# A delta-net stage: U of both blocks made ahead of A, gate decays of the third and last head and one SiLU moved

## Chip, cores and metric

The kernel runs on one core of a Trainium2 chip. The metric is the device time of one execution in microseconds (us). The work is one program with an instruction stream for each engine: TensorE (PE), VectorE (DVE), ScalarE (ACT), GpSimd (POOL) and SyncE (SP). They meet only at semaphores.

## What is computed

Two transformer blocks over 512 tokens of width 1024, all in float32. The change touches only the second block's gated delta rule: 8 heads, key width 128, value width 256, over 528 tokens (16 meta tokens are put ahead). The kernel uses chunks of 128 tokens where the reference has 64, which gives the same result.

```python
def gated_delta_rule(q, k, v, g, beta):
    g = jnp.cumsum(to_chunks(g), axis=-1)
    incl, strict = idx[:, None] >= idx[None, :], idx[:, None] > idx[None, :]
    decay = jnp.exp(jnp.where(incl, g[..., :, None] - g[..., None, :], -jnp.inf))
    kb = k * beta[..., None]
    lower = jnp.where(strict, jnp.einsum('nbhid,nbhjd->nbhij', kb, k) * decay, 0.0)
    rhs = jnp.concatenate([v * beta[..., None], kb * jnp.exp(g)[..., None]], axis=-1)
    sol = lax.linalg.triangular_solve(eye + lower, rhs, left_side=True, lower=True)
    u, w = sol[..., :DV], sol[..., DV:]
    attn = jnp.einsum('nbhid,nbhjd->nbhij', q, k) * decay
    ...
    def step(S, xs):
        v_new = u_c - jnp.einsum('bhcd,bhde->bhce', w_c, S)
        o = einsum(qd_c, S) + einsum(attn_c, v_new)
        S = S * gl_c[..., None, None] + einsum(kd_c, v_new)
        return S, o

# in hybrid_mixer
q = l2norm(heads(jax.nn.silu(causal_depthwise_conv(dq, conv_q)), DN_DK))
k = l2norm(heads(jax.nn.silu(causal_depthwise_conv(dk, conv_k)), DN_DK))
v = heads(jax.nn.silu(causal_depthwise_conv(dv, conv_v)), DN_DV)
o_dn = rmsnorm_2(o_dn, dn_gain) * jax.nn.silu(heads(dz, DN_DV))
```

## The kernel before

**Weights.** Every weight matrix is read from memory in units of 128 output columns. ScalarE rounds a unit to its high part (`w_hi`), VectorE, or in this stage GpSimd, subtracts that from the raw weights (`w_lo`), and TensorE makes three products for each of 8 input tiles. One such input tile is an event ("mm", 8 of them a unit); its six matmuls take about 0.73 us. These products are the bulk of the time, and the delta work is laid between them. Whenever a unit's last tile is issued, ScalarE and GpSimd prepare the unit four further on.

**The order.** `delta_order` (L162) writes the order of events by hand: tables such as `PREPARE`, `DECAYS`, `SCAN`, `L2_FIRST` give each step of a head a time, counted in us of TensorE work (`WORK`, L103) for `steps` and in fill events for `after`, and `timed` (L116) merges them with the product tiles. All engines walk through the same list `DELTA` and each takes its own part of an event, so the list fixes the order on every engine; semaphores do the rest. Iteration i of the loop (0 to 8) scans head i, prepares head i+1, and makes the gate decay and the normed q and k of head i+2.

**A head's preparation.** "bcast" (L2012): ScalarE waits until GpSimd has done with `gB` and `r3` of the head before and issues two DMAs that spread a gate row over 128 partitions. "decay": ScalarE (L2021) makes five Relus, two Exps into `DT`, one Exp of `gB` and a small copy to `gl`; VectorE (L2752) multiplies `DT` by a 0/1 mask (two steps); GpSimd (L3115) makes `LT` from `DT` and the spread row (two steps). "pair" : TensorE (L1380) multiplies k by k and q by k chunk by chunk, first the four chunks of 128 tokens, then the tail of 16; VectorE (L2758) makes from them `UT`, the start of the inverse, and `AT`, the attention matrix. "turn": TensorE (L1395) transposes `UT` of the four chunks, then of the tail; ScalarE copies both back. "x1" to "x6" and "u1" to "u6" double the inverted blocks, with GpSimd making the masked `LM` (L3121), the first right behind "turn".

**A head's scan.** "v0" to "v4" make the new values of a chunk on TensorE, and ScalarE copies them to `V`; "s0" to "s4" update the state `S` and the output; "k1" to "k4" apply the state. "nsq", "norm", "gain0", "gain1", "parts" norm the output and multiply it with SiLU(z), "hiz" splits it in high and low (`oh` on ScalarE, `ol` on GpSimd) for the branch products. "siluqk", "siluv", "siluz" are ScalarE's SiLUs, of which the first after an Exp loads an activation table. `stk0` to `stk2` are VectorE's steps of the norm of k; TensorE waits at "pair" for the last of them. z is kept once, so ScalarE's copy of the next head's z out of PSUM waits until "parts" of this one is done.

**PSUM.** A planner (`Banks.delta`, L969) walks the list too. The chain's small products take four banks in turn from a `Ring` (L413); with each use it notes the semaphore value that tells that the bank's content was read, and the next user of the bank waits for that value beside its own waits. `s.p_u` counts VectorE's eight steps in `pairs` of a head. The product of k and k of the four chunks is ("pair", h, 0), that of q and k ("pair", h, 1), both of the tail are in ("pair", h, 2). In heads 1 to 6 the ring gives ("turn", h, 0) the bank of ("pair", h, 1) and ("turn", h, 1) that of ("pair", h, 2). Head 0 and head 7 fall otherwise: there the transposes take banks that were free before, or that of ("pair", h, 0). The units of products have two pairs of banks of their own, used in turn.

## Time and profile before

| | us |
|---|---|
| median of 3 runs | 2822.25 |
| lowest and highest run | 2819.61, 2822.37 |
| profiled execution, its own time | 2817.93 |
| its span, first to last instruction | 2816.1 |
| delta stage in it | about 1305 to 2000 |
| TensorE busy | 2732.6 (97%) |
| VectorE, ScalarE, GpSimd busy | 1532.0, 1144.8, 472.7 |
| mean granted clock of TensorE | 0.99 |

Times in rows are us from the start of the span unless marked ns. "PE" is TensorE's matmuls, "PEld" its weight loads. A row of a timeline gives start and length; rows that follow one another with the same tiles are merged, and the count stands behind the x. In brackets stands how long the engine was idle before and what ended that. Nearly every VectorE and ScalarE step is recorded by a helper (L481, L486, L492, L474), so the tiles tell which step a row is, out<-in. Granted clock (PEclk) is a share of full speed: 1.00 is 2.4 GHz, 0.50 is 1.2 GHz.

### The profile page before, as it was taken

To read this page: it belongs to the slowest core of one execution; us is meant where nothing else is said; L and a number is where in the kernel's file an instruction comes from. 1 tells how busy PE (TensorE), PEld (TensorE's weight loads), DVE (VectorE), ACT (ScalarE), POOL (GpSimd) and SP (SyncE) were. 2 spreads that over 40 slices of the span, in tenths; PEclk is the share of its full clock that TensorE was granted. 3 is DMA by queue.
4 is the path that set the end of the run, shared out by engine and by line. 5 is a ranking of instruction groups with operands and counts; after the bars stand their busy time and mean duration, and the time that the engine had idled before them with its cause. 6 is when DMAs were issued, how large, how long until landed. Compare 5 with 4: busy or idle time off the path is not lost.

```text
span 2816.1 us, 37383 instructions
## 1 busy us (share of the span) xinstructions
PE 2732.6 (97%) x14573; PEld 2226.4 (79%) x14573; DVE 1532.0 (54%) x2165; ACT 1144.8 (41%) x1709; POOL 472.7 (17%) x278
## 2 busy tenths in 40 slices
PE   8999999998999999998999999999999999999999
PEld 3888888886666788887888888878878877788887
DVE  6735637348667433337645555663367765644443
ACT  4221211226554422235654645554366663432221
POOL 0000000011001000003434444443322222100000
PEclk9999999999999999999999999999999999999999
DMA  6423424222114232323211121211211112332332
GB/s 237 154 88 104 135 75 135 86 67 90 38 46 158 83 98 89 98 90 103 75 40 53 46 68 61 61 48 44 81 55 60 55 60 101 91 100 94 92 101 77
DMA packets 69873, 241.80 MB, mean 86 GB/s; under 512 B 8218, under 2 KB 8346, under 8 KB 69314
## 3 DMA queue, kind: packets, MB, share of 16 engines
q1 hardware_dynamic: 62032, 221.28, 24.6%
q10 hardware_dynamic: 7666, 18.13, 1.9%
q8 instruction: 117, 1.92, 0.3%
q14 instruction: 58, 0.48, 0.1%
HBM read 232.74 MB, written 6.64 MB: 85 GB/s over the span
## 4 chain that ended last, share of the span: by engine, by line
PE 85%; DVE 7%; ACT 6%; issue 1%; DMA 1%; ACTq 0%; DVEq 0%; POOL 0%; SPq 0%; POOLq 0%
PE ps L1115 62%; PE ps L1517 3%; PE ps L1414 2%; PE ps L1618 2%; PE ps L1454 2%; PE ps L1321 1%; PE ps L1342 1%; PE ps L1446 1%; ACT r L474 1%; DVE UT L481 1%; PE ps L1145 1%; ACT w_hi L474 1%; PE ps L1154 1%; DVE f_t L492 1%; PE ps L1475 1%
## 5 line engine op out<-in xcount | busy, mean ns | idle before, releaser
L1115 PE MATMUL ps<-Nh,w_hi 128*128 128x512 f32 (+1 forms) x1808 | 661.3, 366 | 9.6 <-DVE Nl L481 4.9
L1115 PE MATMUL ps<-Nl,w_hi 128*128 128x512 f32 (+1 forms) x1808 | 631.2, 349 | 0.0
L1115 PE MATMUL ps<-Nh,w_lo 128*128 128x512 f32 (+1 forms) x1808 | 628.8, 348 | 0.0
L474 ACT ACTIVATE w_hi<-w_raw 128x1024 fp32r<-128x1024 f32 (+1 forms) x352 | 368.2, 1046 | 633.2 <-PE ps L1115 465.3
L481 DVE TENSOR_TENSOR w_lo<-w_raw,w_hi 128x1024 fp32r<-128x1024 f32 (+1 forms) x242 | 297.7, 1230 | 260.9 <-ACT w_hi L474 250.8
L1115 PEld LDWEIGHTS ps<-Nh,w_hi 128*128 128x128 f32 x1808 | 343.1, 190 | 80.1 <-issue 30.2
L1115 PEld LDWEIGHTS ps<-Nl,w_hi 128*128 128x128 f32 x1808 | 343.4, 190 | 50.6 <-issue 5.8
L1115 PEld LDWEIGHTS ps<-Nh,w_lo 128*128 128x128 f32 x1808 | 343.4, 190 | 44.3
L481 POOL TENSOR_TENSOR w_lo<-w_raw,w_hi 128x1024 fp32r<-128x1024 f32 x110 | 270.4, 2458 | 608.0 <-ACT w_hi L474 604.2
L1115 PE MATMUL ps<-x1h,w_hi 128*128 128x512 f32 (+1 forms) x784 | 272.7, 348 | 11.9 <-ACT x1h L474 8.7
L1115 PE MATMUL ps<-x1l,w_hi 128*128 128x512 f32 (+1 forms) x784 | 267.1, 341 | 0.0
L1115 PE MATMUL ps<-x1h,w_lo 128*128 128x512 f32 (+1 forms) x784 | 265.4, 339 | 0.0
L1115 PEld LDWEIGHTS ps<-x1h,w_hi 128*128 128x128 f32 x784 | 147.5, 188 | 44.4 <-issue 20.9
L1115 PEld LDWEIGHTS ps<-x1l,w_hi 128*128 128x128 f32 x784 | 147.8, 189 | 18.4 <-issue 1.4
L1115 PEld LDWEIGHTS ps<-x1h,w_lo 128*128 128x128 f32 x784 | 147.9, 189 | 18.2 <-DVE w_lo L481 0.2
L481 POOL TENSOR_TENSOR f_t<-f_t,f_t 128x768 f32<-128x768 f32 (+1 forms) x12 | 22.4, 1868 | 658.4 <-ACT f_t L474 658.4
L492 DVE SCALAR_TENSOR_TENSOR ada_acc<-w_raw,sc,ada_acc 128x512 f32<-128x512 f32 x168 | 126.3, 752 | 8.8 <-DVE X L492 0.5
L1115 PE MATMUL ps<-h1h,w_hi 128*128 128x512 f32 x352 | 119.1, 338 | 0.0
L1115 PE MATMUL ps<-h1l,w_hi 128*128 128x512 f32 x352 | 118.9, 338 | 0.0
L1115 PE MATMUL ps<-h1h,w_lo 128*128 128x512 f32 x352 | 117.9, 335 | 0.0
L481 DVE TENSOR_TENSOR f_t<-f_t,ps 128x768 f32<-128x768 f32 (+1 forms) x44 | 36.1, 821 | 141.3 <-PE ps L1115 140.8
L474 ACT ACTIVATE f_t<-ps 128x768 f32<-128x768 f32 (+1 forms) x44 | 31.0, 705 | 150.4 <-PE ps L1115 149.7
(364 smaller groups left out, 4645.1 us busy)
## 6 DMA issues: line engine op xcount, KB each, us to landing
w_raw<-in_w_in SPq DMA_DIRECT2D x132, 512.0 KB, 3.5
w_raw<-in_w_proj SPq DMA_DIRECT2D x89, 512.0 KB, 3.5
w_raw<-in_w_ada SPq DMA_DIRECT2D x52, 512.0 KB, 4.3
w_raw<-in_w_out SPq DMA_DIRECT2D x48, 448.0 KB, 3.3
w_raw<-in_w_out SPq DMA_DIRECT2D x24, 512.0 KB, 3.5
w_raw<-in_w_mix_in SPq DMA_DIRECT2D x19, 512.0 KB, 3.5
w_raw<-in_w_bdn SPq DMA_DIRECT2D x16, 512.0 KB, 3.5
w_raw<-in_w_mix_out SPq DMA_DIRECT2D x8, 512.0 KB, 3.5
```

The source lines that it names most:

```text
L474: self.then_inc(self.e.activation(out, in_, func, **kw), sem)
L481: self.then_inc(self.e.tensor_tensor(out, a, b, op), sem)
L492: self.then_inc(self.e.scalar_tensor_tensor(out=out, in0=a, scalar=s, in1=b, op0=op0, op1=op1), sem)
L1115: ins = e.matmul(out[:, 512 * j:512 * j + n], a[:, kk, :], x[:, kk, c0:c0 + n], start=k == 0 and p == 0, stop=k == nt - 1 and p == 2)
L1145: ins = e.matmul(bank[0:2, 0:512], t.sc[:, 2 * k:2 * k + 2], a[:, i, :], start=k == 0, stop=k == KT - 1)
L1154: ins = e.matmul(bank[0:2, 0:512], t.pick[:, 2 * v:2 * v + 2], t.ada_acc[:, u, v, :], start=v == 0, stop=v == 1)
L1321: ins = e.matmul(out, a[:, k, :], x[:, k, 0:TX], start=k == 0 and p == 0, stop=k == KT - 1 and p == 2)
L1342: ins = e.matmul(out, a[:, kk, :], x, start=i % 4 == 0 and p == 0, stop=i % 4 == 3 and p == 2)
L1414: ins = e.matmul(bank[0:n, c * n:(c + 1) * n], t.LM[lv % 2][0:n, c0 + c, 0:n], UT[0:n, 1, c0 + c, 0:n], start=True, stop=True)
L1454: ins = e.matmul(out, t.Xm[0:n, c0 + c, 0:n], block_columns(UT[0:n, 0, c0 + c, 0:n], lv, 1), start=True, stop=True)
L1517: ins = e.matmul(out[:, 0:TX], a[:, 2 * (k % 4) + x, :], b[:, x, MS], start=x == 0 and p == 0, stop=x == 1 and p == 2)
L1618: ins = e.matmul(out[:, 0:TX], a[:, k, :], b[:, 0, MS], start=p == 0, stop=p == 2)
```

## The change

In `pairs` VectorE makes `UT` of the four chunks and of the tail first, and `AT` of both behind that. The counts that others wait for follow: the transposes and `LM` wait for 8h+3 and 8h+6 or 8h+1 and 8h+4 instead of 8h+7 and 8h+5 for the tail; in the bank plan the release of ("pair", h, 1) goes from value 8h+4 to 8h+7.

The event "decay" is split: "decay" is ScalarE's part alone, and the new event "mask" is VectorE's and GpSimd's. In most heads both stand where "decay" stood. For heads 2 and 7 (`EARLY_DECAYS`, in iterations 0 and 5) "bcast" goes from behind "u6" to behind "v4", "decay" from the end of the iteration to behind "nsq", "mask" stands ahead of "gain0". "pair" of head 7 goes ahead of the first two product tiles of iteration 6. The SiLU of head 2's v goes from the end of iteration 0 to the third product tile of iteration 1, on ScalarE behind the first copy to `V`. No instruction is added or dropped.

```diff
--- before.py
+++ after.py
@@ -64,7 +64,9 @@
 PREPARE = ((1.5, "pair"), (6, "turn"), (9, "x1"), (13, "u1"), (18, "x2"), (23, "u2"),
            (28, "x3"), (33, "u3"), (38, "x4"), (43, "u4"), (48, "x5"), (53, "u5"),
            (61, "x6"), (65, "u6"))
-DECAYS = ((66, "bcast"), (73, "decay"))
+DECAYS = ((66, "bcast"), (73, "decay"), (73, "mask"))
+EARLY_DECAYS = ((46, "bcast"), (53.41, "decay"), (68.4, "mask"))
+FIRST_MASKS = ((25.47, "mask"), (71.65, "mask1"))
 SCAN = ((0.52, "v0"), (5.18, "s0"), (8.86, "k1"), (11.5, "v1"), (14.15, "s1"), (18.33, "k2"),
         (22.47, "v2"), (27.63, "s2"), (30.3, "k3"), (33.44, "v3"), (37.1, "s3"), (38.28, "k4"),
         (45.91, "v4"), (52.07, "s4"), (53.4, "nsq"), (56.65, "norm"), (68.5, "gain0"), (69.6, "gain1"),
@@ -78,12 +80,11 @@
           (27, "stq2"), (39, "l2k"), (42, "lnk"), (48, "stk0"), (48, "stk1"), (48, "stk2"),
           (48, "siluv"))
 L2_FIRST = ((21.01, "siluz"), (22.55, "siluqk"), (25.3, "l2q"), (25.3, "lnq"), (27.1, "stq0"), (30.4, "stq1"),
-            (30.4, "stq2"), (37, "l2k"), (40, "lnk"), (45.3, "stk0"), (45.9, "stk1"), (45.9, "stk2"),
-            (59.1, "siluv"))
+            (30.4, "stq2"), (37, "l2k"), (40, "lnk"), (45.3, "stk0"), (45.9, "stk1"), (45.9, "stk2"))
 L2_LAST = ((18.91, "siluz"), (21.38, "siluqk"), (22.99, "l2q"), (22.99, "lnq"), (25.08, "stq0"), (25.13, "stq1"),
            (27.17, "stq2"), (30.21, "l2k"), (30.71, "lnk"), (30.71, "stk0"), (33.94, "stk1"), (38.5, "stk2"))
 
-LATE_PREPARE = ((1.35, "pair"), (6.9, "turn"), (9.6, "x1"), (11.2, "u1"), (17.7, "x2"), (22.2, "u2"),
+LATE_PREPARE = ((0, "pair"), (6.9, "turn"), (9.6, "x1"), (11.2, "u1"), (17.7, "x2"), (22.2, "u2"),
                 (28.2, "x3"), (32.7, "u3"), (35.7, "x4"), (40.2, "u4"), (46.7, "x5"), (49.7, "u5"),
                 (56.9, "x6"), (60.5, "u6"))
 LATE_SCAN = ((7.95, "v0"), (7.95, "siluv"), (7.95, "s0"), (7.95, "k1"), (9.83, "v1"), (12.1, "s1"),
@@ -165,7 +166,7 @@
     first = products("w_proj", [7 - 5 + j for j in range(3)] + [7 + j for j in range(4)] + [5, 6])
     steps = [(at, s, 0) for at, s in FIRST_STEPS]
     steps += [(at, s, -2) for at, s in FIRST_HEAD] + [(at, s, -1) for at, s in SECOND_HEAD]
-    steps += [(at, s.rstrip("1") if s[0] in "bd" else s, int(s in ("bcast1", "decay1"))) for at, s in FIRST_PREPARE + FIRST_DECAYS]
+    steps += [(at, s.rstrip("1") if s[0] in "bdm" else s, int(s in ("bcast1", "decay1", "mask1"))) for at, s in FIRST_PREPARE + FIRST_DECAYS + FIRST_MASKS]
     out = products("w_proj", [1]) + timed(steps, first)
     for i in range(NH + 1):
         steps = []
@@ -189,9 +190,9 @@
             fills = branches
         if i + 1 < NH:
             steps += [(at, s, i + 1) for at, s in (PREPARE if i + 2 < NH else LATE_PREPARE)]
-        after = []
+        after = [(3, "siluv", 0)] if i == 1 else []
         if i + 2 < NH:
-            steps += [(at, s, i + 2) for at, s in DECAYS]
+            steps += [(at, s, i + 2) for at, s in (DECAYS if 0 < i < NH - 3 else EARLY_DECAYS)]
             after += [(at, s, i) for at, s in (L2_FIRST if i == 0 else L2NORM if i + 3 < NH else L2_LAST)]
         elif i < NH:
             after += [(24.5, "siluz", i)]
@@ -980,7 +981,7 @@
         if name == "columns":
             chain.use(ev, s.gate_col, 6)
         elif name == "pair":
-            for i, v in enumerate((1, 4, 8)):
+            for i, v in enumerate((1, 7, 8)):
                 chain.use((name, h, i), s.p_u, 8 * h + v)
         elif name == "turn":
             for i in range(2):
@@ -1395,7 +1396,7 @@
     def turn(h):
         UT = t.UT[h % 2]
         for i, (c0, n, C) in enumerate(WIDE):
-            w.wait_ge(s.p_u, 8 * h + 4 * i + 3)
+            w.wait_ge(s.p_u, 8 * h + 3 * i + 3)
             bank = ps[:, bank_of(("turn", h, i)), :]
             for c in range(C):
                 ins = e.transpose(bank[0:n, c * n:(c + 1) * n], UT[0:n, 0, c0 + c, 0:n], cs("ident", n, n))
@@ -2756,18 +2757,20 @@
             w.tt(dt, dt, each(cs("incl", n, n), n, C), ALU.mult, s.p_incl)
 
     def pairs(h):
+        def bank(i, j):
+            c0, n, C = WIDE[i]
+            return in_chunks(ps[:, B.of["pair", h, j][0], :] if i == 0 else ps[:, B.of["pair", h, 2][0], j * n:], n, C)
+
         for i, (c0, n, C) in enumerate(WIDE):
-            b, b2 = (in_chunks(ps[:, B.of["pair", h, j][0], :] if i == 0 else ps[:, B.of["pair", h, 2][0], j * n:], n, C)
-                     for j in range(2))
-            dt, at, lt = (a[0:n, c0:c0 + C, 0:n] for a in (t.DT, t.AT[h % 2], t.LT))
-            u = t.UT[h % 2][0:n, 0, c0:c0 + C, 0:n]
+            lt, u = t.LT[0:n, c0:c0 + C, 0:n], t.UT[h % 2][0:n, 0, c0:c0 + C, 0:n]
             w.wait_ge(s.p_lt, 2 * h + i + 1)
             w.wait_ge(s.p_pair, 4 * h + 3 * i + 1)
-            w.tt(lt, lt, b, ALU.mult, s.p_u)
+            w.tt(lt, lt, bank(i, 0), ALU.mult, s.p_u)
             w.tt(u, lt, each(cs("level", n, n, 0), n, C), ALU.mult, s.p_u)
             w.tt(u, each(cs("ident", n, n), n, C), u, ALU.subtract, s.p_u)
+        for i, (c0, n, C) in enumerate(WIDE):
             w.wait_ge(s.p_pair, 4 * h + 2 * i + 2)
-            w.tt(at, b2, dt, ALU.mult, s.p_u)
+            w.tt(t.AT[h % 2][0:n, c0:c0 + C, 0:n], bank(i, 1), t.DT[0:n, c0:c0 + C, 0:n], ALU.mult, s.p_u)
 
     def value_turn(h, i):
         dst, x = ((t.kd, 0), (t.vb, 0), (t.vb, 0), (t.vb, P), (t.vb, P))[i]
@@ -2879,7 +2882,7 @@
             columns()
 
             root(6, f[4], f[0], f[2])
-        elif name == "decay":
+        elif name == "mask":
             decay(h)
         elif name == "pair":
             pairs(h)
@@ -3120,7 +3123,7 @@
 
     def level(h, lv):
         for i, (c0, n, C) in enumerate(WIDE[:XC[lv] - XC[lv - 1]]):
-            w.wait_ge(s.p_u, 8 * h + 4 * i + 1)
+            w.wait_ge(s.p_u, 8 * h + 3 * i + 1)
             if lv > 2:
                 w.wait_ge(s.p_x, 9 * h + min(XC[lv - 3] + i + 1, XC[lv - 2]))
             else:
@@ -3142,7 +3145,7 @@
                 ended = ("w_bdn", 2 * ev[1] + ev[2] // 4)
             continue
         name, h = ev
-        if name == "decay":
+        if name == "mask":
             w.wait_ge(s.r_out, 16)
             decay(h)
         elif name == "turn":
```

## Rows read from the trace of the kernel before

**Rows 1.** Page, section 1: busy time and share of the span, xinstructions.
```profile
PE 2732.6 (97%) x14573; PEld 2226.4 (79%) x14573; DVE 1532.0 (54%) x2165; ACT 1144.8 (41%) x1709; POOL 472.7 (17%) x278
```

**Rows 2.** Waits of PE, 1300 to 2000: us in total, times, longest.
```profile
PE ps L1401 <- DVE AT L481: 6.1, 6, 1.2
...
PE ps L1504 <- ACT r L474: 3.1, 2, 2.1
```

**Rows 3.** Timeline of PE, head 3: start, us, instruction, [idle before <-releaser].
```profile
1569.06 0.61 PE L1401 MATMUL ps<-const,UT 128*128 128x128 f32 x4
1570.88 0.17 PE L1401 MATMUL ps<-const,UT 16*16 16x16 f32 x1 [1.21 <-DVE AT L481]
1570.98 0.40 PE L1115 MATMUL ps<-Nh,w_hi 128*128 128x264 f32 x1
```

**Rows 4.** Timeline of DVE, head 3.
```profile
1567.41 0.69 DVE L481 TENSOR_TENSOR UT<-const,UT 128x512 f32<-128x512 f32 x1
1568.21 0.69 DVE L481 TENSOR_TENSOR AT<-ps,DT 128x512 f32<-128x512 f32 x1
1569.03 0.16 DVE L481 TENSOR_TENSOR LT<-LT,ps 16x16 f32<-16x16 f32 x1
1569.22 1.12 DVE L481 TENSOR_TENSOR UT<-LT,const 16x16 f32<-16x16 f32 x1
...
1570.58 0.16 DVE L481 TENSOR_TENSOR AT<-ps,DT 16x16 f32<-16x16 f32 x1
```

**Rows 5.** Timeline of POOL, head 3.
```profile
1567.63 2.68 POOL L481 TENSOR_TENSOR w_lo<-w_raw,w_hi 128x1024 fp32r<-128x1024 f32 x1 [0.81 <-ACT w_hi L474]
```

**Rows 6.** Timeline of PE, head 2.
```profile
1484.24 0.70 PE L1482 MATMUL ps<-V,kd 128*128 128x256 f32 x2 [4.41 <-ACT V L474]
...
1486.49 0.59 PE L1115 MATMUL ps<-Nh,w_hi 128*128 128x264 f32 x1
```

**Rows 7.** Timeline of ACT, head 2.
```profile
1474.17 2.05 ACT L474 ACTIVATE DT<-gB,gcol 128x128 f32<-128x128 f32 x5
...
1478.13 1.30 ACT L474 ACTIVATE oh<-O 128x512 fp32r<-128x512 f32 x2
...
1481.34 1.28 ACT L474 ACT_TABLE_LOAD   x1
...
1483.81 0.38 ACT L474 ACTIVATE V<-ps 128x256 f32<-128x256 f32 x1
```

**Rows 8.** Timeline of ACT, where it is idle in heads 0 and 5.
```profile
1462.59 0.69 ACT L474 ACTIVATE qk<-ps,const 128x512 f32<-128x512 f32 x1 [4.37 <-PE ps L1497]
...
1872.87 2.08 ACT L474 ACTIVATE r<-ps,const 128x264 f32<-128x264 f32 x4 [2.91 <-PE ps L1504]
```

**Rows 9.** Stretches: A:B us, busy us (x) of PE, PEld, DVE, ACT, POOL; PEclk; DMA.
```profile
1331.46:1334.87 3.41, 3.41 (x18) 3.41 (x17) 3.26 (x3) 3.26 (x5) 1.90 (x1) 0.50 0.07 25
1567.00:1572.00 5.00, 3.72 (x28) 3.20 (x27) 3.79 (x8) 2.09 (x5) 4.05 (x3) 1.00 0.51 125
1898.07:1908.31 10.24, 7.91 (x27) 6.17 (x28) 4.11 (x7) 4.17 (x8) 4.19 (x5) 0.50 0.16 53
```

**Rows 10.** Timeline of PE, head 7.
```profile
1887.60 2.14 PE L1392 MATMUL ps<-qk 128*128 128x128 f32 x20
...
1896.87 0.66 PE L1401 MATMUL ps<-const,UT 128*128 128x128 f32 x4 [3.46 <-DVE UT L481]
1899.31 0.19 PE L1401 MATMUL ps<-const,UT 16*16 16x16 f32 x1 [1.78 <-DVE UT L481]
```

**Rows 11.** Timeline of DVE, heads 0, 3's mask and 5.
```profile
1470.80 1.42 DVE L481 TENSOR_TENSOR O<-O,zz 128x512 f32<-128x512 f32 x2
...
1557.35 2.50 DVE L492 SCALAR_TENSOR_TENSOR vv<-craw,small,vv 128x528 f32<-128x528 f32 x2
...
1885.47 0.71 DVE L492 SCALAR_TENSOR_TENSOR qk<-qk,r 128x528 f32<-128x528 f32 x1
```

**Rows 12.** Timeline of ACT, copy of z in iteration 0.
```profile
1472.30 0.60 ACT L474 ACTIVATE zz<-ps 128x512 f32<-128x512 f32 x1 [2.39 <-DVE O L481]
```

## Prediction

> **What bounds the kernel now.** I read the page first: TensorE is busy for 97% of the span [rows 1], so a step counts only where TensorE stands still or runs at a lower clock. Then the waits of TensorE over the delta phase: the transposes of U wait for VectorE, 6.1 us in six waits for its step A alone [rows 2], and a head's first state product for ScalarE's copy of V. The timelines of TensorE, VectorE, ScalarE and GpSimd around these waits say which head they belong to. Heads 3 to 6 behave alike (1.21 us at the second transpose of each, one of the four in [rows 3]), head 1 waits 1.25 us in two pieces (the rest of the 6.1), head 2 waits 4.41 us for V [rows 6], head 7 waits 3.46 and 1.78 us at its transposes [rows 10]. What is lost beyond the waits is the clock: after a standstill of 2.1 us [rows 2] it was granted at half (1.2 of 2.4 GHz) for 3.41 us, it stayed full through head 3's 1.21 us, and it was half for 10.24 us after head 7's waits [rows 9].
>
> I name VectorE's steps in `pairs` lt, u, u', A: LT times the product, times the level mask, subtracted from the identity, and the attention matrix; 0 is the block of four chunks, 1 the tail of 16 tokens.
>
> **U ahead of A, heads 3 to 6.** Before: u'0 ends at 1568.10, A0 takes 0.69, lt1 follows, and u1 (16x16, 0.16 us by the rows of its kind) takes 1.12 us, up to 1570.34 [rows 4]. In that time GpSimd's w_lo runs from 1567.63 to 1570.31 [rows 5]: u1 reads two SBUF tiles and ends as w_lo ends, while A0 and lt1, which read PSUM, keep their 0.69 and 0.16 beside the same w_lo. So A0 lies today in a stretch in which VectorE would stand still anyway. After the change lt1 comes right behind u'0 (1568.23), u1 stands still until 1570.35 as before, u'1 ends at 1570.54, and only then come A0 (1570.58 to 1571.27) and A1.
> The transposes in the code now wait for U alone, but the bank plan adds a wait: in heads 1 to 6 the first transpose takes the PSUM bank in which the product for A0 lies, and its release moves with A0 from the fourth step to the seventh (`s.p_u` value 8h+7). The second takes the bank of the tail's products, whose last reader is still A1. The first transpose, at 1569.06 today, can thus start only some 0.14 us behind A0 (the lag from A1's end, 1570.74, to the second transpose [rows 3, 4]), at 1571.41. Four transposes and the small one take 0.6 us of issue, so the product tiles go on at 1572.02 and not at 1570.98 (0.10 behind the small transpose [rows 3]): **1.04 us later in each of four heads, +4.2 us**. Behind TensorE in this wait are the product tiles, nothing else hides it. The standstill grows from 1.21 to 1569.23..1571.42, that is 2.19 us (1569.23 is where the product before the first transpose ends). The clock: 2.1 us made it fall, 1.21 did not [rows 2, 3, 9]. A fall of 3.41 us costs up to 1.7. The new value is nearest to the one with a fall, but one case is thin ground: I take two falls in four heads, **+3.2** (bounds 0 and +6.8).
>
> **Head 1.** Here GpSimd has no w_lo beside u1. The three tail steps (lt1, u1, u'1 at 0.2 each with their gaps) move ahead of A0, so the first transpose is 0.6 us later, and the old wait of 0.25 before the second is won back: **+0.3**. Head 0: no bank hangs on A there, but u1 again stands beside a w_lo and ends with it, so the second transpose starts when it did: **0**.
>
> **Head 2, decay and SiLU moved.** ScalarE reaches V's copy at 1483.81 though V's product is done at 1475.5. Ahead of it in its queue lie the decay (1474.17 to 1478.10) and table load and SiLU of V (1481.34 to 1483.7) [rows 7]. The decay (3.93 us) goes to the idle of 4.37 us before 1462.59 [rows 8]; it fits with 0.4 to spare. Its two broadcast DMAs take 0.8 us of ScalarE's queue near 1452, where nothing is waiting for it; they land long before 1458. The SiLU with its table load goes behind the copy. V is then copied by 1483.81 - 3.93 - 2.4 = 1477.5, plus what follows, well before TensorE asks for it. So the 4.41 us vanish. What is late next is VectorE. The mask now stands before the gains: 0.96 us of its own (0.69 and 0.16 with their gap), and GpSimd's LT right behind it holds up the next two-tile step, as it does in head 3, where two taps take 2.50 us [rows 11] where two steps without it take 1.54: 1.9 us in all. The products with SiLU(z) end at 1472.22 today [rows 11]; ScalarE's copy of z waits for them and ends 1472.90 [rows 12], and unit 19 needs that copy's bank at 1474.15. With 1.9 us more the copy ends at 1474.8 and TensorE loses 0.8 us. The transpose then is set by VectorE: lt0 at 1478.0 (1.15 us after the pair products start), u0 at 1478.72. GpSimd is ready for ol at 1478.79. If u0 comes first, A0 ends at 1483.2 and tiles go on at 1483.9 (today 1486.49 [rows 6], and at half clock for 2.0 us more, another 1.0): -3.6. If ol comes first, u0 and u'0 each stand behind one ol and u1 behind a w_lo, A0 ends at 1485.4, tiles go on at 1486.2: -0.3. The two differ by 0.07 us of estimated time; I take the middle, **-2.0**.
> The Trainium skill, page "SBUF — State Buffer", section "SBUF: two separate sides", says that of a VectorE step with two SBUF inputs and a GpSimd step that reads SBUF the one that starts first has the shared ports for its whole instruction and the other is blocked. Taken at its word with my instants u0 is first and head 2 gives -3.6, and the total would be 1.6 us lower; the 1.12 us of u1 agree with it [rows 4].
>
> **Head 7.** The decay (3.9 us) goes to an idle stretch of 2.91 us [rows 8], 1.1 too short: ScalarE's next chain, which ends in the copy that TensorE already waits 0.5 us for, is 1.1 us later. The mask again adds 1.9 us to VectorE ahead of the last k scaling, whose end at 1886.18 was 1.4 us before the pair product (1887.60) [rows 10, 11]; the product now stands two tiles earlier, at 1887.0, and needs that scaling at 1889.2, or at 1891.3 if the w_lo of about 1888.3 gets in front of it. TensorE stands still for 2.3 to 4.4 us there. The seven tiles that follow keep it busy to 1896.6 or, at half clock, 1900.4. VectorE's u'0 comes at 1898.9 in both cases (today 1896.82), u1 and A0 at 1900.1 and 1901.0, and V's first product at 1901.15 (today 1899.43): 1.7 us later. Against it stands the clock: today it is half from 1898.07 to 1908.31 [rows 9]; at full speed the steps from the transposes to the first u product take 5.5 us, not 9.1 (each product half as long, the waits for copies unchanged), 3.6 us back. Net **-1.9** (bounds +1.7 with a slow clock again, -4.3 with the scaling in time).
>
> **Sum.** 0 + 0.3 - 2.0 + 4.2 + 3.2 - 1.9 = +3.8. The profiled execution took 2817.9 (span 2816.1) and becomes 2821.7; the median of the runs is 2822.25, 4.3 above it, so 2826.0.
>
> **Rivals.** (1) *The early decays pay in full.* Head 2 loses its whole standstill and half clock less the 0.8 (-4.6), head 7 its two transposes' waits and the clock (-5.2 - 3.6, +1.1 from the crowded ScalarE): -7.7; with +4.5 of heads 1 and 3 to 6 and no clock falls that is -7.8, **2814.5**. For it: the masks are done some 9 us sooner, and [rows 6, 7] show ScalarE as the one that ends last in head 2. Against it: VectorE's two-tile steps still meet the same GpSimd work. Where A0 in heads 3 to 6 costs nothing at all, -4 more. (2) *The clock falls each time.* The 2.2 us standstill at the first transpose of heads 3 to 6 drops the clock in all four: 4.2 + 6.8, head 1 +0.3, head 2 -0.3 and head 7 0: +11.0, **2833**. It decides from the third fall on, or from two with head 7 at +1.7: above 5.6 the kernel counts as slower. (3) *No clock falls*: 0.3 - 2.0 + 4.2 - 1.9 = +0.6, **2822.9**. (4) *The bank wait does nothing*, because TensorE comes to the transpose later than I think: 0.3 - 2.0 - 1.9 = -3.6, **2818.7**, the same verdict as mine.
>
> **How the numbers follow.** About 0.2% (5.6 us) is what a measurement of this kernel can tell from no change. My forecast, within 5.6 us and slightly up: 0.35; rival 3, 0.15; rival 4, 0.07: together 0.57 for no change. Rival 1: 0.15, faster. Rival 2 and its smaller forms: 0.28, slower. The range runs from 2816.5 to 2832.5: below it lies about half of rival 1, above it the far end of rival 2.
>
> **What would show it.** In heads 3 to 6 the first transpose waits some 2.2 us, for A of VectorE, with no wait at the second; A0 follows the 1.1 us u1. In head 2 the wait for V is gone, the copy of V lies about 1479.5, and a wait of 0.8 appears at unit 19 for the z copy. In head 7 a wait of 2 to 4 us for VectorE's scaling stands ahead of the pair products. I am wrong if the first transposes of heads 3 to 6 start where they did, if u1 is short when it comes first, or if the sum of the two early heads gives more than 6 us.

## The result, and the profile after

| | before | after |
|---|---|---|
| median (lowest to highest), us | 2821.12 (2819.61 to 2822.37) | 2830.23 (2828.63 to 2831.4) |
| span of the profiled execution, us | 2816.1 | 2828.5 |
| ratio to before | 1 | 1.0028, 95% interval 1.0019 to 1.0038 |

The change makes the kernel 0.28% slower, 9.1 us by the medians. The time lies in my range (2816.5 to 2832.5), 4.2 us above my 2826.0; of the three directions I had given the most to no change (0.57), and it is slower (0.28).

The waits of TensorE from 1300 to 2000 us, after the change (engine, line, what was waited for: us in total, times, longest), answer to [rows 2]:

```profile
PE ps L1402 <- DVE AT L482: 16.1, 6, 5.8
PE ps L1393 <- DVE qk L493: 4.3, 1, 4.3
...
PE ps L1402 <- DVE UT L482: 2.5, 2, 1.8
PE ps L1455 <- ACT Xm L475: 1.7, 1, 1.7
...
PE ps L1483 <- ACT V L475: 1.2, 2, 0.7
```

The wait for V's copy has gone (1.2 us left of 5.4), and so have the two waits for U at head 7's transposes. The transposes wait for A instead, 16.1 us where it was 6.1, and in head 7 there is a new wait for the k scaling (qk, 4.3) and a longer one for Xm. First head 3; its three timelines in turn, TensorE, VectorE and GpSimd, answer to [rows 3], [rows 4] and [rows 5] (start us, us, instruction, idle time before it and its releaser in brackets):

```profile
1573.26 1.21 PE L1402 MATMUL ps<-const,UT 128*128 128x128 f32 x5 [2.17 <-DVE AT L482]
```

```profile
1569.27 0.69 DVE L482 TENSOR_TENSOR UT<-const,UT 128x512 f32<-128x512 f32 x1
...
1570.29 1.90 DVE L482 TENSOR_TENSOR UT<-LT,const 16x16 f32<-16x16 f32 x1
...
1572.42 0.89 DVE L482 TENSOR_TENSOR AT<-ps,DT 128x512 f32<-128x512 f32 x2
```

```profile
1569.49 2.67 POOL L482 TENSOR_TENSOR w_lo<-w_raw,w_hi 128x1024 fp32r<-128x1024 f32 x1 [0.81 <-ACT w_hi L475]
```

This is the picture I had drawn: w_lo runs to 1572.16, u1 ends at 1572.19, A0 follows, and the first transpose starts 0.15 us behind A0's end (1573.11). All five transposes now stand in one row, with one wait ahead of them and none at the second. The other three heads show the same 2.17 us. Then the clock, in stretches right behind three of these waits, or beginning in them, and one behind head 6's (columns as in [rows 9]; the last three values are the granted clock, the DMA share and GB/s):

```profile
1572.79:1579.62 6.83, 6.37 (x27) 5.85 (x27) 1.39 (x4) 0.77 (x2) 2.50 (x4) 0.50 0.23 77
1661.54:1664.95 3.41, 3.41 (x14) 3.32 (x15) 0.00 (x0) 0.70 (x2) 1.48 (x2) 0.50 0.33 132
1746.87:1750.28 3.41, 3.20 (x14) 2.87 (x15) 0.65 (x3) 0.77 (x2) 2.24 (x4) 0.50 0.51 154
...
1833.00:1836.40 3.40, 3.27 (x25) 3.06 (x26) 0.99 (x3) 0.77 (x2) 2.18 (x4) 1.00 0.52 159
```

Three of the four heads fall to half clock (0.50, 1.2 of 2.4 GHz), one for 6.83 us, and the fourth does not. Such a stretch at half clock is called a clock fall below.

Where the time went, read from when each stage starts in the two timelines (V's first product v0 of each head, minus the same in before): up to v0 of head 1 +0.23; head 2 +1.64; heads 3, 4, 5 +3.93, +2.69, +2.50, with a clock fall each; head 6 +1.08 up to its transposes, without one; from there to v0 of head 7 another +0.62; sum +12.7, and the span is 12.4 longer. The medians differ by 9.1: the profiled execution of before was a fast one (2817.93, its median is 2821.12), that of after lies at its median (2830.34, 2830.23), so some 3 of the 12.4 us are the choice of execution.

Head 2. TensorE, GpSimd, VectorE and ScalarE after the change, answering to [rows 6], [rows 7] and [rows 12]:

```profile
1486.74 1.21 PE L1402 MATMUL ps<-const,UT 128*128 128x128 f32 x5 [5.79 <-DVE AT L482]
```

```profile
1475.39 2.63 POOL L482 TENSOR_TENSOR w_lo<-w_raw,w_hi 128x1024 fp32r<-128x1024 f32 x1 [14.89 <-ACT w_hi L475]
1478.18 1.64 POOL L482 TENSOR_TENSOR LT<-DT,r 128x512 f32<-128x512 f32 x2 [0.17 <-POOL w_lo L482]
```

```profile
1479.50 0.69 DVE L482 TENSOR_TENSOR LT<-LT,ps 128x512 f32<-128x512 f32 x1 [3.72 <-POOL LT L482]
```

```profile
1473.56 0.60 ACT L475 ACTIVATE zz<-ps 128x512 f32<-128x512 f32 x1 [2.79 <-DVE O L482]
...
1478.57 0.38 ACT L475 ACTIVATE V<-ps 128x256 f32<-128x256 f32 x1
```

ScalarE did what it should: V is copied at 1478.57. The mask was done at 1470.4, but GpSimd had stood idle for 14.89 us and then ran w_lo first, since LT is behind it in its queue, and this w_lo waits for w_hi, that for the copy of z. LT starts at 1478.18, later than before (1477.73), so lt0 is later, too, and behind it come the 1.90 us u1 and A. The clock was half for 6.83 us from 1484.05 on; in the trace of before it was half for 3.41, from 1485.06 on.

Head 7, TensorE and VectorE:

```profile
1905.15 1.22 PE L1393 MATMUL ps<-qk 128*128 128x128 f32 x4 [4.26 <-DVE qk L493]
```

```profile
1898.88 0.96 DVE L482 TENSOR_TENSOR DT<-DT,const 128x512 f32<-128x512 f32 x2
1899.87 2.46 DVE L493 SCALAR_TENSOR_TENSOR O<-O,small,r 128x512 f32<-128x512 f32 x2
1902.36 2.73 DVE L493 SCALAR_TENSOR_TENSOR qk<-qk,r 128x528 f32<-128x528 f32 x1
```

The last k scaling takes 2.73 us where it took 0.71 [rows 11], since a w_lo runs on GpSimd from 1902.11 to 1904.53, and TensorE waits 4.26 us for it. The scaling itself starts 1.47 us behind the end of TensorE's last product (1900.89), since the mask (1898.88) and the O steps beside LT (2.46 us) stand ahead of it. The longer wait is the 1.7 us for ScalarE's copy `Xm`, 0.5 before.

### The profile page after: what moved, and what is told of

It reads as the page before. It is cut to its first block, busy times and chain, and to the rows that moved or that the text cites. A ratio compares the mean times of both kernels' runs of the same rounds, so it can differ in the third digit from the quotient of the medians.

```text
span 2828.5 us, 37369 instructions
## 1 busy us (share of the span) xinstructions
PE 2737.9 (97%) x14573; PEld 2233.4 (79%) x14573; DVE 1537.2 (54%) x2165; ACT 1144.8 (40%) x1709; POOL 472.3 (17%) x278
## 4 chain that ended last, share of the span: by engine, by line
PE 84%; DVE 8%; ACT 6%; issue 1%; DMA 1%; POOL 0%; ACTq 0%; DVEq 0%; SPq 0%; POOLq 0%
PE ps L1116 61%; PE ps L1518 3%; PE ps L1415 2%; PE ps L1619 2%; PE ps L1455 1%; PE ps L1322 1%; PE ps L1343 1%; PE ps L1447 1%; DVE UT L482 1%; ACT r L475 1%; ACT w_hi L475 1%; PE ps L1146 1%; PE ps L1155 1%; DVE f_t L493 1%; ACT DT L475 1%
```

## The experiments

Ratios are to the kernel before, timed with it on the same chip; the first number is the kernel's own median, the brackets hold the ratio's 95% interval. A ratio of 0.001 is 2.8 us. Besides the medians I read from each trace what happened in the stage in question, since a median moves with clock falls elsewhere. The executions of the kernel before alone lie between 2815.36 and 2826.81 us.

**The reorder alone, and the moves alone.** The first is the kernel before with the diff's `pairs`, its wait values and bank plan; the second is the kernel after with the old `pairs`:

```diff
-            for i, v in enumerate((1, 4, 8)):
+            for i, v in enumerate((1, 7, 8)):
-            w.wait_ge(s.p_u, 8 * h + 4 * i + 3)
+            w.wait_ge(s.p_u, 8 * h + 3 * i + 3)
```

> The kernel before with one part of the change: U of both blocks ahead of A, the counts that follow from it and the later release of the bank; no event is moved. Theory 1 (the bank's release behind A, with VectorE's tail step standing behind GpSimd's w_lo, costs 1.04 us in each of heads 3 to 6, and the 2.1 us standstills let TensorE's clock fall): first transposes of heads 3 to 6 wait 2.1 us each, no wait at the second, half clock behind at least two of the four, +7 to +11 us over before, that is nearly all of the +9.1 of the whole change. Rival (the moved events cost the time, above all the 4.26 us standstill ahead of head 7's pair product and the 5.76 us in head 2): here at most +4.5 us, and the rest is in moves_only.

> The changed kernel with VectorE's old order in pairs (A of a block right behind its U) and the old bank release; the early broadcasts, decays and masks of heads 2 and 7, the moved SiLU and the earlier pair of head 7 stay. Theory 1: heads 3 to 6 wait 1.2 us at the second transpose again; head 2 waits some 4 us at its first and second transpose together instead of 4.41 for V; head 7 stands still about 4.3 us ahead of the pair products; sum -2 to +2 us over before. Rival (the moved events cost the time): +5 to +8 us.

Reorder alone: 2829.15 us, 1.0019 (1.0011 to 1.0028), the larger part of the loss: 7.0 of 9.1 us by the medians, 0.19 of 0.28% by the ratios (5.4 us, under the +7 to +11 that I expected). The waits at the first transposes of heads 3 to 6 are 2.15 to 2.17 us; head 3 without a clock fall costs 1.10 us, the others, with 6.83, 3.41 and 3.41 us at half clock, more.

Moves alone: 2819.69 us, 0.9994 (0.9985 to 1.0003), no difference that can be measured. Its TensorE shows why:

```profile
1483.31 0.63 PE L1402 MATMUL ps<-const,UT 128*128 128x128 f32 x4 [3.44 <-DVE AT L482]
1485.14 0.18 PE L1402 MATMUL ps<-const,UT 16*16 16x16 f32 x1 [1.20 <-DVE AT L482]
...
1892.32 4.00 PE L1393 MATMUL ps<-qk 128*128 128x128 f32 x20 [4.26 <-DVE qk L493]
```

Head 2's 4.41 us for V are 4.64 us for A. Head 7 has 1.72 and 4.26 in the place of 0.47, 3.46 and 1.78. Between v0 of head 5 and v0 of head 7 it is 0.65 us slower than before. The two halves add up to 3.7 us by the ratios, the whole is 7.9; the three intervals, each about 2.5 us either way, leave open whether they cost more together than apart. Head 2's 5.79 us wait, 4.64 without the reorder, is one place where they do.

**A0 ahead of u1, in two orders.** Both are the kernel before with another order of VectorE's eight steps: lt0, u0, u'0, lt1, A0, u1, u'1, A1 (A in the gap), and lt0, u0, u'0, A0, lt1, A1, u1, u'1 (the steps that read PSUM first). The edit of the second:

```diff
             w.tt(lt, lt, b, ALU.mult, s.p_u)
+            if i:
+                w.tt(at, b2, dt, ALU.mult, s.p_u)
             w.tt(u, lt, each(cs("level", n, n, 0), n, C), ALU.mult, s.p_u)
```

> The kernel before with VectorE's order lt0, u0, u'0, lt1, A0, u1, u'1, A1: U of the tail is begun before A of the four chunks, but A0 stands ahead of the step that meets w_lo. Theory 1 (A0 reads PSUM and is free while w_lo holds up u1): u1 starts 0.7 us later than in reorder_only and ends at the same time, with w_lo; the first transposes do not wait; time as before, -0.5 to +1 us. Rival (any step put between u'0 and A0 costs its length, the lock has no part in it): +0.3 us per head, and u1 still takes 1.1 us or moves its end by 0.2.

> The kernel before with order lt0, u0, u'0, A0, lt1, A1, u1, u'1: the two tail steps that read PSUM come first, the two that read only SBUF last. Theory 1: A1's 0.2 us go into the time in which u1 would wait for w_lo; u1 begins 0.2 us later and ends with w_lo as before; the second transposes of heads 3 to 6 start 0.2 us earlier (wait 1.0 instead of 1.21), -0.2 us in each of heads 3 to 6 and in 0 and 7, -1 us in all, too little to be told by the clock time but to be seen in the trace. Rival (u1 simply takes 1.1 us as the first tail step on SBUF): the second transpose starts when it does before, or 0.2 later.

A in the gap: 2823.27 us, 0.9999 (0.9987 to 1.0012). PSUM first: 2822.34 us, 1.0000 (0.9991 to 1.0008). The second transposes of heads 3 to 6 wait 0.98 us in the one and 0.92 in the other (1.21 before). With A in the gap the first transpose of head 3 comes 0.2 us later behind the product ahead of it, 0.15 us after A0 ends (1572.59, 1572.74), and the head gains nothing; with PSUM first the first transposes don't wait and a head is up to 0.3 us shorter. VectorE and GpSimd in head 3, PSUM first:

```profile
1569.54 0.69 DVE L481 TENSOR_TENSOR AT<-ps,DT 128x512 f32<-128x512 f32 x1
...
1570.76 0.92 DVE L481 TENSOR_TENSOR UT<-LT,const 16x16 f32<-16x16 f32 x1
```

```profile
1568.98 2.67 POOL L481 TENSOR_TENSOR w_lo<-w_raw,w_hi 128x1024 fp32r<-128x1024 f32 x1 [0.81 <-ACT w_hi L474]
```

u1 takes 1.90, 1.12, 1.19 or 0.92 us by when it is issued, and ends 0.03 us behind w_lo each time (here 1571.68 and 1571.65). In all four orders that begin with lt0, u0 and u'0, u1 is issued behind w_lo's start and ends with it; they differ in what stands behind it. An order with u1 between u0 and u'0 was not run. The gain of 0.3 us a head does not reach the medians.

**w_lo cut short.** The reorder alone, with GpSimd's one step beside u1 made on an eighth of its columns:

```diff
+                k = 1 if n in (191, 199, 207, 215) else KT
-                w.tt(t.lo[n % PARTS][:], t.raw[ring(SPLITS[n])[0]][:], ...
+                w.tt(t.lo[n % PARTS][:, 0:k, :], t.raw[ring(SPLITS[n])[0]][:, 0:k, :], ...
```

> The reorder alone (both blocks' U ahead of A), and GpSimd's one w_lo step that runs beside VectorE's steps in each of heads 3 to 6 is made on one eighth of its columns (the rest of those four tiles keeps old values, so the low parts of four branch weights are not computed). Theory L (u1 waits for w_lo, and A0 behind it holds the bank of the first transpose): u1 falls from 1.90 to about 0.2 us, A0 starts 0.8 us behind u'0, the wait at the first transpose of heads 3 to 6 falls from 2.13 to 0.3 to 0.6 us, no clock fall in these heads, and the time is 2 to 5 us under before (that is 7 to 11 under the reorder with its w_lo). Rival D (TensorE waits because eight steps in the new order are too long, whoever runs beside them): the wait stays over 1.2 us and the time is over before's.

This kernel leaves out the low parts of four branch weights. 2822.15 us, 1.0008 (0.9999 to 1.0018): each taken against before, 6.5 us under the reorder by the medians and 3 by the ratios, whose intervals overlap. In the trace no clock fall stands in heads 3 to 6, but the wait is 1.50 us and not 0.3 to 0.6, and the time is not under before's. By these two numbers rival D's forecast came, by the steps it did not. VectorE and GpSimd, head 3:

```profile
1569.18 0.16 DVE L481 TENSOR_TENSOR UT<-LT,const 16x16 f32<-16x16 f32 x1
1569.38 1.25 DVE L481 TENSOR_TENSOR UT<-const,UT 16x16 f32<-16x16 f32 x1
1570.66 0.89 DVE L481 TENSOR_TENSOR AT<-ps,DT 128x512 f32<-128x512 f32 x2
```

```profile
1568.41 0.76 POOL L481 TENSOR_TENSOR w_lo<-w_raw,w_hi 128x128 fp32r<-128x128 f32 x1 [0.82 <-ACT w_hi L474]
1569.34 3.26 POOL L481 TENSOR_TENSOR LM<-LT,const 128x512 f32<-128x512 f32 x4 [0.17 <-DVE UT L481]
```

u1 is short now, as the theory wants. But GpSimd, free early, starts LM, its next step, at 1569.34, in the 0.04 us between u1 and u'1; its first piece takes 1.27 us, up to 1570.61, and u'1 ends at 1570.63. That a GpSimd step holds the tail up is borne out, against rival D; that w_lo is the only one that can was wrong.

**Head 2 with LT ahead in GpSimd's queue.** The moves of head 2 alone, the mask set two tiles earlier:

```diff
-EARLY_DECAYS = ((46, "bcast"), (53.41, "decay"), (68.4, "mask"))
+EARLY_DECAYS = ((46, "bcast"), (53.41, "decay"), (66, "mask"))
```

> Kernel before with the moves of head 2 alone (broadcast, decay and mask of head 2 early, SiLU of head 0's V behind the copy of V), and with head 2's mask set before the first product tile of unit 12, so that GpSimd's LT stands in its queue ahead of the w_lo step that waits for the copy of z. In the kernel with all the moves and the old order, LT stood behind that w_lo (1477.10), lt0 came at 1478.41, and the transposes of head 2 waited 3.41 and 1.17 us where before V was waited for 4.41: nothing gained. Theory Q (GpSimd's queue holds LT back): LT now ends before 1472, lt0 starts 1.15 us behind the start of the pair products, and the two waits sum to 2.0 to 2.8 us; time 1.8 to 2.6 us under before. Rival P (the wait is set by VectorE's steps standing beside GpSimd's ol and w_lo, whenever LT comes): lt0 comes earlier but u and u' take longer, the sum of the waits stays above 3.8 and the time is within 0.7 us of before.

2824.03 us, 1.0004 (0.9995 to 1.0012). TensorE and VectorE:

```profile
1476.20 0.36 PE L1116 MATMUL ps<-Nh,w_hi 128*128 128x264 f32 x1 [1.08 <-ACT zz L475]
1483.36 0.63 PE L1402 MATMUL ps<-const,UT 128*128 128x128 f32 x4 [0.53 <-DVE AT L482]
1486.40 0.17 PE L1402 MATMUL ps<-const,UT 16*16 16x16 f32 x1 [2.41 <-DVE AT L482]
```

```profile
1479.32 0.69 DVE L482 TENSOR_TENSOR LT<-LT,ps 128x512 f32<-128x512 f32 x1 [1.63 <-PE ps L1393]
...
1483.74 2.32 DVE L482 TENSOR_TENSOR UT<-const,UT 16x16 f32<-16x16 f32 x1
```

LT ran at 1471.22, lt0 starts 1.15 us behind the pair products, and the waits fall from 4.64 to 2.94 us: the queue had held LT back. (I had expected 2.0 to 2.8, and a time 1.8 to 2.6 us under before, which the median does not show.) Against it stands the wait of 1.08 us for the copy of z. From v0 of head 1 to v0 of head 2 the kernel is 1.37 us shorter than before; that is under what its median can show. u'1 was issued 0.04 us behind a w_lo (1483.70) and took 2.32 us.

**Head 7 with decay and mask elsewhere.** The moves of head 7 alone, with

```diff
-EARLY_DECAYS = ((46, "bcast"), (53.41, "decay"), (68.4, "mask"))
+EARLY_DECAYS = ((46, "bcast"), (62, "decay"), (70.4, "mask"))
```

> Kernel before with the moves of head 7 alone, changed: the decay stands in ScalarE's idle stretch of 4.81 us that ends at 1884.63 and not in the one of 2.91 us, and the mask stands behind the last k scaling. In the kernel with all the moves TensorE waited 1.72 us (before 0.47) for the copy Xm and 4.26 us for the k scaling, and head 7 as a whole was 0.65 us longer than before. Theory K (the two waits come from where decay and mask were put): Xm's wait is back at 0.47 us, the wait for the k scaling is under 0.6, the waits at the two transposes (3.46 and 1.78 before) sum to 2.5 to 4.2 us, and the time is 1 to 2.7 us under before. Rival P (the k scaling is late whatever stands ahead of it, since the pair product comes two tiles earlier): a wait of 1.5 us or more for the scaling remains and the time is within 1 us of before.

2822.45 us, 0.9999 (0.9990 to 1.0008). TensorE:

```profile
1884.59 1.10 PE L1456 MATMUL ps<-UT,Xm 128*128 128x64 f32 x8 [0.48 <-ACT Xm L476]
1890.99 2.25 PE L1394 MATMUL ps<-qk 128*128 128x128 f32 x20 [0.25 <-DVE qk L494]
1898.99 0.66 PE L1403 MATMUL ps<-const,UT 128*128 128x128 f32 x4 [0.69 <-DVE UT L483]
1902.63 0.18 PE L1403 MATMUL ps<-const,UT 16*16 16x16 f32 x1 [2.98 <-DVE UT L483]
```

Each wait is where theory K put it: the long waits for Xm and for the scaling were made by where decay and mask stood. The time is not: it gains 1.6 us at the transposes, loses 0.25 ahead of the pair and 1.1 in a wait before the first product that reads S, which grew from 0.62 to 1.69 us; from v0 of head 5 to v0 of head 7 0.2 us are left. The profile names no releaser for that wait, but VectorE and GpSimd show it:

```profile
1902.87 4.17 DVE L494 SCALAR_TENSOR_TENSOR vv<-craw,small,vv 128x528 f32<-128x528 f32 x3
1907.17 0.42 DVE L488 TENSOR_SCALAR S<-ps 128x256 f32<-128x256 f32 x1
```

```profile
1902.72 4.39 POOL L483 TENSOR_TENSOR LM<-LT,const 128x512 f32<-128x512 f32 x4 [0.17 <-DVE UT L483]
```

TensorE's products ahead of the new S end at 1906.00, but VectorE is still in three steps of v beside GpSimd's LM, makes S from 1907.17 to 1907.59, and TensorE goes on at 1907.70. In the kernel before S started at 1903.29, 0.10 us behind these products. And u'1, at 1900.25, was issued 0.04 us behind a w_lo (1900.21) and took 2.32 us, which is why 2.98 us are left at the second transpose.

**The tail's steps first.** If whatever follows w_lo is late, the tail's steps can go ahead of it. TensorE makes the 16x16 products first, VectorE lt1, u1, u'1, A1, lt0, u0, u'0, A0. The second kernel also has the pair products of heads 1 to 6 one product tile earlier, the third has only this shift, in heads 3 to 6, with the old order:

```diff
-        for i, (c0, n, C) in enumerate(WIDE):
+        for m, i in enumerate((1, 0)):
+            c0, n, C = WIDE[i]
...
-PREPARE = ((1.5, "pair"), (6, "turn"), ...
+PREPARE = ((1, "pair"), (6, "turn"), ...
```

> Kernel before with VectorE's tail steps first: TensorE makes the two 16x16 products ahead of the large ones, VectorE does lt1, u1, u'1, A1 and then lt0, u0, u'0, A0; the attention of scan and transposes wait for their own steps, the bank plan follows. No 16x16 step of VectorE then stands beside GpSimd's w_lo. Theory L (u1, a step with two SBUF inputs, stands still until w_lo ends, and this alone makes the 1.18 us at the second transpose of heads 3 to 6, and 2.13 with the reorder): if u'0 starts ahead of w_lo the four waits of 1.18 fall below 0.3 and the time is 4 to 6 us under before; if w_lo starts first (u0 ends within 0.1 us of its start by the rows of before) u'0 stands until w_lo ends, the first transpose of each of these heads waits 1.5 to 2.3 us and the time is 2 to 8 us over before. Rival D (TensorE waits because VectorE has too much to do between product and transpose, whoever shares its ports): the order of blocks changes nothing, each wait stays between 0.9 and 1.4 us and the time within 2 us of before.

> As the kernel with the tail steps first, and the pair products of heads 1 to 6 one product tile (1.1 us) earlier, the transposes where they were. Theory L: all eight steps of VectorE end before w_lo starts, the waits at the transposes of heads 3 to 6 fall below 0.2 us, no clock fall between 1500 and 1880, and the time is 4.5 to 7 us under before. Rival D: some 1.1 us of each wait goes, too, by the earlier start alone, but u'0 and A0 keep their durations whether w_lo runs or not; it is told from L by the run with the tail first and the pair where it was. Rival E (the pair products one tile earlier wait for the scaled q or k, or for their banks): a new wait of 0.3 to 1 us ahead of the pair products of each head, time within 2 us of before.

> Kernel before, its order of VectorE's steps unchanged, with the pair products of heads 3 to 6 one product tile (1.1 us) earlier and the transposes where they were. Control for the kernel with the tail steps first and the pair early, where the waits of heads 3 to 6 vanished. Theory L (the tail's u1 cannot start while w_lo runs, so its end is w_lo's end): the wait at the second transpose stays at 1.1 to 1.3 us in each of heads 3 to 6, time within 1.5 us of before. Rival D (1.1 us more for VectorE is what counts): the wait falls below 0.3 us and the time by 3.5 to 5 us.

Tail first: 2842.27 us, 1.0067 (1.0054 to 1.0079), the slowest of all and far over the 2 to 8 us that I had put for its worse branch. Its VectorE and GpSimd in head 3:

```profile
1571.10 1.96 DVE L481 TENSOR_TENSOR UT<-LT,const 16x16 f32<-16x16 f32 x1
...
1574.28 2.49 DVE L481 TENSOR_TENSOR UT<-LT,const 128x512 f32<-128x512 f32 x1
1576.80 1.64 DVE L481 TENSOR_TENSOR UT<-const,UT 128x512 f32<-128x512 f32 x1
```

```profile
1570.67 2.37 POOL L481 TENSOR_TENSOR w_lo<-w_raw,w_hi 128x1024 fp32r<-128x1024 f32 x1
1573.87 2.35 POOL L481 TENSOR_TENSOR w_lo<-w_raw,w_hi 128x1024 fp32r<-128x1024 f32 x1 [0.83 <-ACT w_hi L474]
1576.39 3.77 POOL L481 TENSOR_TENSOR LM<-LT,const 128x512 f32<-128x512 f32 x4 [0.17 <-POOL w_lo L481]
```

I had reckoned with one w_lo and there are two: u1 now fell into the one before, the rest slid 2 us, u0 fell into the second and u'0 into LM. The waits are 3.0 us in each of the four heads, with a clock fall at or behind each. With the shift (2821.66 us, 0.9997, 0.9988 to 1.0006) the waits of heads 3 to 6 are gone altogether, and the loss is in head 0 (3.58 us at the transposes where it was 2.5), head 7 (5.95 for 5.24) and in head 2 (2.2 us, though it waits for V as before: the clock is half for 6.83 us behind that wait and not for 3.41, and for 3.41 more at 1540.26). I had expected 4.5 to 7 us under before. The shift alone (2821.16 us, 1.0000, 0.9991 to 1.0008) leaves them at 1.18 to 1.20 us: room for VectorE alone is worth nothing, since u1 still ends with w_lo.

**The gains together.** Tail first and the shift in heads 3 to 6 only; then with head 2's moves as above:

```diff
+TAIL_FIRST = (3, 4, 5, 6)
-                steps += [(at, s, i + 1) for at, s in (PREPARE if i + 2 < NH else LATE_PREPARE)]
+                steps += [(1 if s == "pair" and i + 1 in TAIL_FIRST else at, s, i + 1)
+                          for at, s in (PREPARE if i + 2 < NH else LATE_PREPARE)]
```

> Kernel before with the tail's steps first and the pair products one tile early in heads 3 to 6 alone; heads 0 to 2 and 7 as before, where tail first cost 2.4, 1.4 and 2.5 us. Theory L: no wait over 0.2 us at the transposes of heads 3 to 6, 1.1 us less in each, no clock fall between 1500 and 1880 of the kind that one head in four showed: time 3.5 to 5.5 us under before. Rival E (moving the heads' work against the other units brings a new wait or a clock fall elsewhere, as the one near 1550): time within 2 us of before.

> As the kernel with the tail first in heads 3 to 6, and with head 2's decay, mask and SiLU moved and its LT ahead of the w_lo in GpSimd's queue, which made head 2 1.4 us shorter by its trace. If the two gains add: 5 to 7 us under before and 1 to 2 under the kernel without the moves of head 2; if head 2's gain is not there in the median: within 0.7 us of that kernel.

The first: 2817.51 us, 0.9983 (0.9975 to 0.9992). The second: 2814.31 us, 0.9980 (0.9968 to 0.9991), **faster than before, and by the two ratios some 13 us faster than the kernel after**, with which it was not timed side by side. Both are about as fast as expected (3.5 to 5.5 and 5 to 7 us under before; 4.8 and 5.6 by the ratios), though clock falls did come in heads 3 to 6. VectorE, GpSimd and TensorE of the second in head 3:

```profile
1564.06 0.18 DVE L484 TENSOR_TENSOR UT<-LT,const 16x16 f32<-16x16 f32 x1
...
1565.62 1.67 DVE L484 TENSOR_TENSOR UT<-LT,const 128x512 f32<-128x512 f32 x1
1567.33 0.69 DVE L484 TENSOR_TENSOR UT<-const,UT 128x512 f32<-128x512 f32 x1
```

```profile
1564.36 2.38 POOL L484 TENSOR_TENSOR w_lo<-w_raw,w_hi 128x1024 fp32r<-128x1024 f32 x1
1567.57 2.68 POOL L484 TENSOR_TENSOR w_lo<-w_raw,w_hi 128x1024 fp32r<-128x1024 f32 x1 [0.82 <-ACT w_hi L477]
```

```profile
1569.00 0.71 PE L1401 MATMUL ps<-const,UT 128*128 128x128 f32 x5
```

u1 ends and u'1 begins ahead of the first w_lo, u'0 starts 0.24 us ahead of the second and keeps its 0.69, and no wait stands ahead of the transposes. Only u0 still pays. The margin is thin: by these rows, with 0.24 us more ahead of u'0 the w_lo would be first. That head 2's moves add to it stands in the traces alone: head 2 is 1.39 us shorter than in before and 2.35 shorter than in the first of the two (by the starts of v0); the two medians differ by 3.2, and the intervals overlap.

## Why the prediction was right and wrong

**Heads 3 to 6, the standstill: right.** Forecast 2.19 us at the first transpose and none at the second, 1.04 us later per head; measured 2.17, none, and 1.08 in the head without a clock fall. The runs with A0 ahead of u1 show its cause: the 2 us wait at the first transpose is there only where A0 stands behind u1, and the transpose starts 0.15 us behind A0 in both the kernel after and the one with A in the gap.

The page "SBUF — State Buffer" of the Trainium skill, section "SBUF: two separate sides", has the first to start, of a VectorE step with two SBUF inputs and a GpSimd step that reads SBUF, keep the shared ports. The runs agree: u'0 issued 0.22 to 0.24 us ahead of w_lo kept 0.69 us, u'1 issued 0.04 behind it took 2.32.

**The clock: right in kind, mis-sized.** I took two falls, +3.2. In the profiled execution there were three, one twice as long. With 1.08 for the wait, heads 3, 4 and 5 leave 2.85, 1.61 and 1.42: +5.9. That is rival 2 but for head 6. The condition that I had named for it ("from the third fall on") is what happened.

**Head 2: wrong.** Forecast -2.0 (-3.6 to -0.3), measured +1.64. The wait for V did vanish and V's copy came at 1478.57, nearly 1 us ahead of what I said. The step that failed is that GpSimd's LT runs "right behind" the moved mask: I moved the mask on VectorE and took LT along with it. GpSimd's LT stayed behind a w_lo that waits, over w_hi and the copy of z, for the very gains that the mask delays. The same error gave the 0.8 us wait at unit 19: it was 0.14, because LT was not there to hold up the gains; with LT ahead in the queue it was 1.08. Then the price of LT being late: u0, u'0 and u1 stand behind ol and w_lo, which was my case of -0.3, but 1.5 us later still, and A0 behind u1 adds its own, 5.79 for 4.64 us without the reorder.

Not all of the +1.64 is the change. In nine other kernels head 2 waits its 4.4 us for V as before; behind that wait eight of them show 6.83 us at half clock and only one the 3.41 of before's trace. In five of the eight, those without a further fall near 1540, head 2 is 0.96 to 1.02 us longer than in that trace. Measured against these, the moved head 2 loses some 0.6 us and not 1.6. The forecast of a gain stays wrong.

**Head 7: right in mechanism, wrong in the sum.** Forecast -1.9 (-4.3 to +1.7), measured +0.6. The standstill ahead of the pair products (4.26, forecast 2.3 to 4.4) and ScalarE's chain 1.1 later (1.72 for 0.47) came as put down; so did the two waits' end. What failed is the term "3.6 us back" of the clock: before, it was half for 10.24 us once; after, for 3.41 (1893.65) and 6.83 us (1903.89), the same in all. The new waits, 1.72 us up to 1893.20 and 4.26 up to 1905.15, each came with a fall, as the old ones had.

**Heads 0 and 1.** Forecast 0 and +0.3. Together +0.23, but from two larger terms: +1.12 by v0 of head 0, a stretch in which the clock was half for 6.83 us and not 3.41, and a fall near 1458 that did not come again, in this or any other of the kernels.

By the terms: the predicted sum +3.8 became +12.4 by +3.6 in head 2, +2.7 in the clock of heads 3 to 6 and +2.5 in head 7, with 0.2 the other way. No one term turned the direction. The runs say it in two halves: the moves, from which I expected -3.9 us, gain nothing that can be measured (-1.7 by the ratio), and the reorder costs 5.4 to 7.0, for which I had put 7.7 with heads 1 and 3 to 6.

That the time lies in my range is in part luck. The terms were wrong by 8.6 us in the traces, nearly all one way; added to the base of 2822.25 the measured +12.4 would have been 2834.7, above the range. The medians lie only 9.1 apart, because the execution that the terms were read from was some 3 us faster than before's median.

## What to carry to other kernels

When a step moves on one engine, write down its followers on every other engine and look at what stands ahead of each in that engine's queue; a producer that is 7 us earlier (here the mask, 7.5) gains nothing when its consumer is queued behind a step that waits for something else. A small VectorE step with both inputs in SBUF costs what is left of the GpSimd step that runs beside it, so put it ahead of that step's start or leave nothing behind it; look for the GpSimd step before, and the one after, too. A standstill that TensorE's clock answers should be priced with its fall each time, and a gain from a fall that goes away only if no new standstill takes its place.

## What the runs showed that I had not expected

A waiting GpSimd step gets in between two VectorE steps that are 0.03 to 0.04 us apart: LM at 1569.34 between u1 (ends 1569.34) and u'1, w_lo at 1483.70 between u1 (ends 1483.70) and u'1, and w_lo at 1900.21 between the same two in head 7 (u1 ends 1900.22). The second of them then took 1.25, 2.32 and 2.32 us for its 0.16.

Clock falls don't only follow standstills. With waits of 2.15 to 2.17 us in heads 3 to 6 it fell in six of eight cases, in them or behind them, with 3.0 us in four of four, and with 0.9 to 1.5 us in none. The length of the last wait does not settle it: in head 1 the clock stayed full behind 1.61 us (1410.18, kernel after) and fell 1.2 us behind one of 1.46 (1413.18, tail first). And the kernel with the shift alone, the one with head 2's moves and the one with head 7's show 3.41 us at half clock twice in mid-head, where TensorE was without a wait over 0.4 us for dozens of us:

```profile
1619.60:1623.01 3.41, 3.41 (x17) 3.31 (x16) 3.07 (x4) 0.68 (x2) 3.02 (x2) 0.50 0.55 154
```

The trace of before has none there, but one of the same kind at 1457.75, in head 1. Each costs some 1.6 us (in that kernel v0 of head 3 comes 1.57 us later by it), which is as much as most terms of this case; why they come is open. A trace is one execution, and those of one kernel differ by up to 11 us (2815.36 to 2826.81), so a trace's span says little; only the rows around a step do.
